# The experts' gate weights (w3) loaded from ScalarE's queue instead of SyncE's

## The reference, cut to what matters

```python
def hier_moe(h, w_group, b_group, w_expert, b_expert, w1, w3, w2):
    ...                       # choose 2 of 64 experts for each token, sort the tokens by expert
    def expert_block(args):
        xb, e = args          # tokens of one expert
        return (jax.nn.silu(xb @ w1[e]) * (xb @ w3[e])) @ w2[e]
    ...                       # weigh and add the two results of each token

def first_block(x, c, ...):
    ...
        h2 = rms_norm(x, norm2_w[l]) * (1 + sc2) + sh2
        x = x + g2 * hier_moe(h2, w_group[l], b_group[l], w_expert[l], b_expert[l], w1[l], w3[l], w2[l])
    return x
```

## Time and profile before

| what | value |
|---|---|
| time, median of 3 runs | 2044.81 us (2043.11 to 2046.37) |
| profiled execution, span | 2044.9 us |
| busy: PE, PE weight loads | 1769.7 us (87%), 1124.1 us (55%) |
| busy: DVE, ACT | 660.9 us (32%), 244.3 us (12%) |
| bytes moved by DMA | 589.8 MB, mean 288 GB/s |
| of these by SP's queue (q1), by ACT's queue (q10) | 581.8 MB, 7.4 MB |
| expert stage, 336.7 to 1420.5 us | 1083.8 us at 360 GB/s |

### The profile page before, as it was taken

One profiled execution on the slowest core, in us unless ns is written; L12 is line 12 of the kernel. 1 busy time (PEld: TensorE's weight loads), 2 busy tenths in 40 slices (PEclk: granted clock), 3 DMA queues, 4 the chain that ended last, 5 costly groups with the idle time before them and its releaser, 6 DMA issues.

```text
span 2044.9 us, 26701 instructions
## 1 busy us (share of the span) xinstructions
PE 1769.7 (87%) x11391; PEld 1124.1 (55%) x11391; DVE 660.9 (32%) x1044; ACT 244.3 (12%) x466; POOL 5.0 (0%) x10
## 2 busy tenths in 40 slices
PE   5987888898898888888889788888778899979997
PEld 4876764343434343333434343433666699968997
DVE  2564434101001010101010110101543777757775
ACT  2013230010101010100101010100132200021001
POOL 0000000000000000000000000000000000000000
PEclk8988899999999999999999999999899899989999
DMA  9799844999999999999999999999395255523552
GB/s 364 267 335 387 292 165 142 358 373 364 353 378 355 372 337 375 356 362 353 357 356 372 345 367 359 352 377 348 131 343 187 99 207 189 188 98 124 185 185 82
DMA packets 258730, 589.80 MB, mean 288 GB/s; under 512 B 6864, under 2 KB 17264, under 8 KB 258560
## 3 DMA queue, kind: packets, MB, share of 16 engines
q1 hardware_dynamic: 253792, 581.82, 77.6%
q10 hardware_dynamic: 4896, 7.37, 1.1%
HBM read 586.55 MB, written 2.62 MB: 288 GB/s over the span
## 4 chain that ended last, share of the span: by engine, by line
PE 39%; DMA 32%; issue 9%; SPq 7%; PEld 6%; DVE 5%; ACT 2%; DVEq 0%; PEldq 0%; ACTq 0%
DMA ring<-in_w 30%; SPq L375 6%; PE ps L1372 4%; PE ps L1772 4%; PE ps L1773 4%; PE ps L1777 4%; PEld ps L1637 4%; PE ps L1621 4%; PE ps L1533 3%; PEld ps L1602 2%; PE ps L1791 2%; PE ps L1790 2%; PE ps L1788 2%; PE ps L1316 1%; DMA ring<-in_w_ada 1%
## 5 line engine op out<-in xcount | busy, mean ns | idle before, releaser
L1621 PE MATMUL ps<-ring,mixT 128*64 128x512 f32 x2048 | 465.5, 608 | 75.5 <-DMA ring<-in_w 74.0
L1621 PEld LDWEIGHTS ps<-ring,mixT 128*64 128x64 f32 x2048 | 158.5, 139 | 357.3 <-issue 347.4
L1637 PE MATMUL ps<-ring,arena 128*64 128x512 f32 x1024 | 241.3, 625 | 44.7 <-DMA ring<-in_w 35.1
L1048 DVE TENSOR_TENSOR arena<-arena,ps 128x512 f32<-128x512 f32 x32 | 22.0, 688 | 608.4 <-PE ps L1621 608.4
L709 DVE TENSOR_TENSOR ring_parts<-ring,ring_parts 128x1024 fp32r<-128x1024 f32 (+3 forms) x119 | 189.7, 1626 | 1.0
L1637 PEld LDWEIGHTS ps<-ring,arena 128*64 128x64 f32 x1024 | 87.3, 144 | 178.1 <-issue 178.1
L1772 PE MATMUL ps<-mixT_parts,ring_parts 128*128 128x256 f32 x704 | 172.9, 283 | 6.7 <-issue 6.7
L1773 PE MATMUL ps<-mixT_parts,ring_parts 128*128 128x256 f32 x704 | 172.4, 283 | 0.0
L1043 DVE COPY mixT<-ps 128x1024 f32<-128x1024 f32 x33 | 40.4, 1225 | 344.1 <-PE ps L1602 344.1
L1772 PEld LDWEIGHTS ps<-mixT_parts,ring_parts 128*128 128x128 f32 x704 | 134.5, 191 | 8.1 <-issue 7.2
L1602 PEld LDWEIGHTS ps<-arena,xn 128*128 128x128 f32 x1056 | 120.4, 192 | 27.9 <-issue 27.9
(11 more groups left out here) (344 smaller groups left out, 1534.3 us busy)
## 6 DMA issues: line engine op xcount, KB each, us to landing
ring<-in_w SPq DMA_DIRECT2D x192, 2048.0 KB, 19.1
ring<-in_ada_w SPq DMA_DIRECT2D x24, 2048.0 KB, 13.3
ring<-in_f SPq DMA_DIRECT2D x22, 2048.0 KB, 7.9
ring<-in_w_ada SPq DMA_DIRECT2D x12, 2048.0 KB, 15.9
ring<-in_f SPq DMA_DIRECT2D x22, 1024.0 KB, 5.0
ring<-in_w_in SPq DMA_DIRECT2D x5, 2048.0 KB, 17.3
ring<-in_w_out SPq DMA_DIRECT2D x2, 2048.0 KB, 9.0
ring<-in_mix_in SPq DMA_DIRECT2D x2, 2048.0 KB, 11.9
```

The source lines that it names most:

```text
L1621: last = mm(ps[half[u], j, :], XeT[:, k, half[u]], w[u][:, k, :], start=(k == 0), stop=(k == KD - 1))
L1637: last = mm(ps[half[u], m, :], heT[:, k, half[u]], w[u][:, k, m * 512:(m + 1) * 512], start=(k == 0), stop=(k == FE // P - 1))
```

## The change

SP's expert loop skips the two w3 loads of the pairs 0 to 31 (`first`). ACT issues them through a new function, `w3_loads`, with the same waits on `ring_used`, the same slots and the same landing semaphores. For pair 0 it is called once, ahead of ACT's expert loop, behind the last part of the second norm (`norm_out(1, 4)`). For pair i + 1 it is called in the loop's turn i between the Silu and the copy. The last turn has no next pair and stands outside the loop. The overflow pairs (`later`) keep all six loads on SP; they do not run with these inputs.

```diff
             def expert_loads(S, pair, i):
 
                 for j, (w, k) in enumerate((("w1", KD), ("w3", KD), ("w2", FE // P))):
+                    if j == 1 and S is first:
+                        continue
                     for u in range(2):
...
+            def w3_loads(i):
+
+                for u in range(2):
+                    n = RE + 2 + u
+                    act.wait_ge(ring_used, n + 1 if isinstance(i, int) else i * NS + (n + 1))
+                    src = A["w3"][bass.ds(i * 2 + u, 1)].rearrange("e (k p) n -> p (e k) n", p=P)
+                    dst = chunk_slot(n).rearrange("p (k n) -> p k n", k=KD)
+                    act.dma_start(dst, src).then_inc(loaded[n % NS], 16)
...
             norm_out(1, 4)
+            w3_loads(0)
             act.wait_ge(lg_mm, 1)
...
-            def expert_pair(S, i):
+            def expert_pair(S, i, more=False):
                 act.wait_ge(S.h1, i + 1)
                 nc.scalar.activation(gsil, ps[:, 0, :], ACT.Silu).then_inc(S.silu, 1)
+                if more:
+                    w3_loads(i + 1)
                 act.wait_ge(S.y, i + 1)
                 nc.scalar.activation(Ye, ps[:, 0:2, :].rearrange("p b n -> p (b n)"), ACT.Copy).then_inc(S.yc, 1)
 
-            with act.Fori(0, E // 2) as i:
-                expert_pair(first, i)
+            with act.Fori(0, E // 2 - 1) as i:
+                expert_pair(first, i, True)
+            expert_pair(first, E // 2 - 1)
```

## The result

The changed kernel takes 2279.72 us (median; 2276.85 to 2283.0), beside 2045.59 us for the kernel before on the same chip. The ratio is 1.115, with a 95% interval of 1.113 to 1.117. The forecast was 2263 us, the range 2215 to 2325. The profiled execution has a span of 2275.0 us.

A forecast was written before the change was run, and what follows sets the result against it. DMA looked like the bound, but a chain through w3's landing set the 34.92 us period. New period 0.14 + 24.5 + 0.2 + 14.48 + 0.95 + 1.69 = 41.96 us, 7.04 more 31 times: 2263 us, range 2215 to 2325.

The forecast's parts named there:

- Equal shares for the two queues: Behind each release, w1 and w3 queues alternate packet by packet, so both finish together at the end of four transfers.
- the wait moved from w3 to w1: PE's DMA wait stands ahead of the w1 matmuls, 8 to 9 us each, some 260 us in all.
- w2 hidden: On SP's queue w2 follows w1, lands by 35 us, and PE wants it at 42 or later.
- The chain before: Old expert period: issue, w3's landing, w3's matmuls, DVE's product and release form one closed chain of 34.9 us.
- issue to the second w1 landing: In each new period, the four w1 and w3 loads end 24.5 us after issue; upper bound 26.8.
- w1, transposes, w3 at full clock: PE runs both groups and the transposes behind the landing in 14.48 us, as in pair 0.
- low clock in w1's group: After 8.4 us of PE idle, w1's group runs partly at 1.2 GHz, costing 1.69 us; bounds 0.8 and 3.4.
- 402 GB/s: Rate taken for both queues active, at which the four loads take 20.9 us and end at 24.3.
- the forecast's 0 for it: Pair 0's two w3 loads on ACT cost nothing, landing about 311 us, before their matmuls at about 328.5.
- Order kept: Rival: w1 still lands early enough and w3 stays the chain's link; 2020 us, or 2045 without better rate; 4 in 100.
- ACT comes late: Rival: ACT issues w3 some microseconds behind SP, shortening the period by the lag; 3 us gives 2170 us; 3 in 100.
- Longer low clock, same mechanism: Rival: w3's group on low clock too, 1.69 us more per period, 2315 us; 12 in 100 shared with lower rate.

The follow-up runs named there:

- experiment 1: Changed kernel, with ACT waiting for the first w1 load's landing before issuing w3, and SP for the first w3 load's before w2: 2113.65 us.
- experiment 2: Kernel before, with all six loads of pairs 1 to 31 on ACT's queue, order w1, w3, w2 kept: 2042.93 us, ratio 0.9987.
- experiment 8: Changed kernel, with SP's w1 loads for the next pair released as soon as the w1 matmuls are done; w3 stays on ACT: 1969.39 us.
- Experiment 9: Kernel before, all loads on SP, with w1, w3 and w2 each released behind h1, h3 and y of the pair before: 1954.82 us.
- experiment 3: Kernel before, with only w2 moved to ACT's queue behind the copy; w1 and w3 stay on SP in order: 2390.85 us, ratio 1.169.
- experiment 6: Kernel before, with w1 moved to ACT's queue and w3 and w2 left on SP, pairs 1 to 31: 2374.04 us, ratio 1.161.
- experiment 7: Changed kernel, with SP waiting for the landing of the pair's second w3 load before it issues w2: 2277.11 us.

## Why the prediction was right

**The mechanism.** Equal shares for the two queues, w1 landing near the end of all four transfers, the wait moved from w3 to w1, w3 free of waits, w2 hidden: each was read in the profile after as it had been foretold. Experiments 1, 2 and 8 show the cause from both sides. Order restored gives back 166 us with both queues in use; ACT's queue alone with the order kept costs nothing; with a lead for w1 the split kernel is 76 us faster than the kernel before.

Two details were wrong, and neither is on the chain. w3 was to land with w1, at 24 to 25 us, and landed at 28: the prediction let w2 follow w1 on SP's queue, but not take turns with w3's last packets. And the packets of the two queues were not equal in the first 4 us behind a release, since ACT's queue started late.

**The chain before.** That the period before was one chain of issue, start of the queue, transfers, w3's matmuls and release, and not a full set of engines, was the base of the sum. Experiment 9 bears it out: with w1 issued 8.3 us earlier, and w3 and w2 released early as well, each period was 2.7 us shorter, though the DMA share had read 0.97 before.

**The terms.** By the chain's own parts, the new period was forecast as 41.96 us and measured as 42.62:

| term, us | forecast | measured |
|---|---|---|
| release to issue | 0.14 | 0.14 |
| issue to the second w1 landing | 24.5 | 24.4 to 25.0, 24.75 in the mean |
| landing to PE | 0.2 | 0.06 |
| w1, transposes, w3 at full clock | 14.48 | 14.48 |
| low clock in w1's group | 1.69 | 2.26 |
| to the next release | 0.95 | 0.95 |

The term that was mis-sized is the low clock. The forecast took the one row of before, 8.78 us, as the price of each group, with 3.4 us as the upper bound. In fact the w1 groups ran 8.43 to 10.08 us, 9.35 in the mean, and most periods alternate between about 42.1 and 43.2 us. The row of before was seen behind 3 us of idle, in 7 of 31 groups; behind 8.8 us all 31 were on the low clock for a time. But the length of the idle time does not set the size: groups of 8.8 and of 9.9 us stand behind the same 8.7 to 9.0 us of idle, the 12 us of experiments 3 and 6 gave 9.25 and 9.22 us, and in experiment 9 the w2 groups took 7.85 us in the mean behind 1.2 us. What sets it is open. The difference, 2.26 - 1.69 = 0.57 us, makes 18 us in 31 periods, most of the 21 us by which the stage came out longer than forecast.

**The rate and the start.** The landing was set by 402 GB/s, read in a stretch where the second queue wrote to HBM. The measured rate of the two queues together was 387 GB/s, as with one. The rule of the Trainium skill ("DMA: Bandwidth & Descriptors", section "Rules for kernel authors"), that several issuing engines bring no bandwidth, was right against the row that I took. By that rate the four loads should have ended at 25.1 us. In experiment 7, where w2 does not share, the last of them ends at 25.7 us in the mean, so start and completion took 4.0 us and not 3.4. The second w1 load is there 1.0 us before it, since SP's queue got ahead: by 321 - 119 = 202 packets of 2 KB (last section), 1.1 us at 387 GB/s. That the landing was off by only 0.25 us, 8 us in all, is luck: a rate and a start taken too well, against a lead of w1 that the sum did not have.

**The sum against the time.** The stage grew by 1321.36 - 1082.43 = 238.9 us; the parts ahead of it and behind it are 4.8 and 4.0 us shorter, so the span grew by 230.1. The first release came at 328.6 to 335.0 us in the profiled executions of the ten experiments, with pair 0's w3 loaded from SP in five of them and from ACT in the others, and both kinds spread over this range. So the 4.8 us are no effect of that edit that these runs can show, and the forecast's 0 for it stands. Nor was the time of the profiled execution that of the median: its span is 2275.0 us, 4.7 us less. The forecast was 17 us low in all: 21 us in the stage, less the 8.8 us outside it that were put at nothing, plus these 4.7. The range, too, was drawn narrower than its terms: with the stated bounds, 26.8 us for the landing and 3.4 for the low clock, the period would be 45.97 us and the upper end 2387 us. The time fell inside the narrower one.

**The rivals.** "Order kept" was not seen. "ACT comes late" was true in small: ACT issued w3 0.02 us ahead of SP, but its queue started 2 us later, which put w1 1.0 us ahead of w3. "Longer low clock, same mechanism" was partly true, for w1's group and not for w3's.

## What to carry to other kernels

Two DMA queues on one set of engines gave no more bandwidth here (387 GB/s with one and with two) and took away an order: loads that start together end nearly together, at the time of the last. Before moving a load to a second queue, find which load the chain waits for, and see what will take turns with it; even a load that nobody needs yet (w2 in experiment 3) does the damage. Where DMA looks full and a wait is left, release each buffer when its own reader is done, before thinking of another queue: here that was worth 91 us.

## What the runs showed of the hardware that was not expected

**A queue that starts while the other has work starts late.** When both queues start at one time from empty, SP's gets going first. From 1016 to 1020 us in the changed kernel, just behind a release (the DMA table again):

```profile
DMA packets 440, 0.90 MB, mean 225 GB/s; under 512 B 0, under 2 KB 0, under 8 KB 440
...
q1 hardware_dynamic: 321, 0.66, 61.8%
q10 hardware_dynamic: 119, 0.24, 19.4%
```

The issues were within 0.03 us of each other. By the packets' own start times, SP's queue moved its first packet 1.1 us behind its issue and ACT's 3.1 us, in the mean of 31 periods. It is no property of ACT's queue. The one ACT load of experiment 2 that was issued with both queues empty (332.2 us) moved its first packet after 1.07 us. And SP's queue is late in its turn: its w2 loads, issued to an empty queue while ACT's w3 loads ran, took 3.4 us to the first packet in experiment 1 and 3.5 us in experiment 8. One of these, and the DMA table of experiment 8 for 1057.8 to 1061.4 us, in which q1 has no row:

```profile
L380 SPq DMA_DIRECT2D ring<-in_w x1: 372/372/372, 1057.7 to 1057.7; - x1
...
DMA packets 688, 1.39 MB, mean 386 GB/s; under 512 B 9, under 2 KB 9, under 8 KB 688
...
q10 hardware_dynamic: 688, 1.39, 105.0%
```

It is no rule without exception: a load of another tensor on ACT's queue, issued at 250.9 us in the kernel before while SP's queue had work, moved its first packet after 1.14 us. What holds the second queue up, and why SP's is the first of two that start together, is open.

**The queues share by packets, not by bytes.** w2's packets have 4 KB and w3's 2 KB. With w2 on SP and w3 on ACT there were 137 against 132 packets, 0.54 against 0.27 MB, from 1038.5 to 1040.5 us in the changed kernel:

```profile
q1 hardware_dynamic: 137, 0.54, 68.6%
q10 hardware_dynamic: 132, 0.27, 35.6%
```

With the roles exchanged, w2 on ACT and w3 on SP, it was the same, from 1037 to 1043 us in experiment 3:

```profile
q10 hardware_dynamic: 394, 1.59, 67.6%
q1 hardware_dynamic: 395, 0.81, 35.2%
```

So the queue with the larger packets gets the larger part of the rate. What this adds in experiment 3 can be estimated. At 1035 us, when w2's first packet moves, 3.6 MB of w3 are left on SP's queue, and they are through at 1055.4. With equal bytes for both queues at 400 GB/s (the rate of that table) they would take 2 x 3.6 / 0.400 = 18 us, some 2 us less.
